# A two-layer attention, state-space and gated linear attention trunk: the first output projection in split fp32r products, its weights split in turns of the attention loop

## The reference, cut to what matters

```python
# layer 0
h = x @ w_in                                   # cq, ckv, k_rope, g_mla, u, g_s5
o_mla = mla_attention(...) * silu(g_mla)       # 8 heads, 512 channels, causal softmax
y = gelu(s5(u))
o_s5 = y * sigmoid(y @ w_glu + b_glu) * silu(g_s5)          # 256 channels
z = concatenate([o_mla, o_s5]) @ w_out         # 768 x 1024: the first output projection
x = layer_norm(ALPHA * x + z)
# layer 1
h = x @ w_in                                   # q, k, v, gk_low (16 columns), g
log_a = log_sigmoid(gk_low @ w_gk2 + b_gk) / 16             # the gate products, 16 x 512
o = rms_norm(chunked gated linear attention(q, k, v, log_a)) * silu(g)
x = layer_norm(ALPHA * x + o @ w_out)
```

## Time and profile before

| | us |
|---|---|
| median of 3 runs | 928.06 (923.01 to 928.16) |
| profiled execution | 926.22 |
| its span | 924.5 |
| attention turns 4 to 63 | from about 202 to 385 |
| first output projection | 385 to 475 |

### The profile page before, as it was taken

How to read it: one execution, slowest core, us unless ns; L and a number is a source line. 1 busy time by engine, 2 the same in 40 slices (tenths; PEclk the granted TensorE clock), 3 DMA queues, 4 the chain that set the end, 5 groups by cost and what they waited for, 6 DMA issues and landing times. The chain is left out here.

```text
span 924.5 us, 11820 instructions
## 1 busy us (share of the span) xinstructions
PE 892.7 (97%) x4384; PEld 691.5 (75%) x4384; DVE 448.1 (48%) x787; ACT 273.7 (30%) x536; POOL 222.0 (24%) x245
## 2 busy tenths in 40 slices
PE   7999999999999999999998999999999999999995
PEld 6888776766788777744455877888888888888884
DVE  5988689456666898344440433100000025554453
ACT  6152414553433344211113445002020326211120
POOL 2000002411110100544443230033413333142243
PEclk9999999999999999999999999999999999999998
DMA  9010255220000000522213110021001332021111
GB/s 338 11 28 23 72 84 121 85 76 2 1 1 1 1 1 13 170 77 83 91 57 103 46 46 1 11 86 52 23 23 50 98 114 92 23 81 57 46 48 67
DMA packets 34888, 55.61 MB, mean 60 GB/s; under 512 B 7664, under 2 KB 21232, under 8 KB 34816
## 3 DMA queue, kind: packets, MB, share of 16 engines
q1 hardware_dynamic: 34832, 54.87, 19.5%
HBM read 43.78 MB, written 9.44 MB: 58 GB/s over the span
## 5 line engine op out<-in xcount | busy, mean ns | idle before, releaser
L1521 DVE SCALAR_TENSOR_TENSOR w_out_lo<-w_out_raw,vecs,w_out_hi 128x1024 fp32r<-128x1024 f32 x8 | 10.5, 1314 | 161.8 <-ACT w_out_hi L1131 161.6
L1812 PEld LDWEIGHTS psum<-V,probT 128*128 128x128 f32 x576 | 69.3, 192 | 11.7 <-issue 8.1
L1812 PE MATMUL psum<-V,probT 128*128 128x64 f32 x576 | 74.4, 275 | 0.3 <-DVE rot L1468 0.3
L1675 PE MATMUL psum<-kT,qTt 96*128 96x512 f32 (+3 forms) x192 | 72.5, 487 | 1.2 <-DVE YT L612 1.2
L1063 ACT ACTIVATE prob<-psum,negmax 128x128 f32<-128x128 f32 (+7 forms) x64 | 47.4, 740 | 81.6 <-DVE negmax L1423 71.0
L1423 DVE TENSOR_REDUCE negmax<-psum 128x1 f32<-128x128 f32 (+7 forms) x64 | 48.5, 758 | 29.8 <-PE psum L1679 28.4
L1588 PE MATMUL psum<-w_out,OT 128*128 128x512 f32 x128 | 57.6, 593 | 0.0
L1588 PE MATMUL psum<-x1T_hi,wqk_hi 128*128 128x512 f32 x128 | 51.2, 400 | 0.0
L1588 PE MATMUL psum<-x1T_lo,wqk_hi 128*128 128x512 f32 x128 | 50.8, 397 | 0.0
L1588 PE MATMUL psum<-x1T_hi,wqk_lo 128*128 128x512 f32 x128 | 50.6, 395 | 0.0
L1588 PE MATMUL psum<-w_out_hi,Y1T_hi 128*128 128x512 f32 x128 | 50.6, 395 | 0.0
(11 more groups left out here) (349 smaller groups left out, 1923.7 us busy)
## 6 DMA issues: line engine op xcount, KB each, us to landing
wqk_raw<-odd_w_in_dram SPq DMA_DIRECT2D x8, 512.0 KB, 5.3
x_res<-x_dram SPq DMA_DIRECT2D x8, 512.0 KB, 3.4
x_scratch<-zn SPq DMA_DIRECT2D x8, 512.0 KB, 2.6
wv_raw<-odd_w_in_dram SPq DMA_DIRECT2D x16, 256.0 KB, 2.7
wg_raw<-odd_w_in_dram SPq DMA_DIRECT2D x16, 256.0 KB, 2.7
w_out_raw<-odd_w_out_dram SPq DMA_DIRECT2D x4, 1024.0 KB, 5.0
V<-x_scratch SPq DMA_DIRECT2D x8, 512.0 KB, 4.2
out_dram<-SG SPq DMA_DIRECT2D x8, 512.0 KB, 2.9
```

The costliest lines, as they stand in the source:

```text
L1521: step(vec.scalar_tensor_tensor(w_out1[2][:, k, :], w_out1[0][:, k, :], gla_c[:, 4 + k % 2:5 + k % 2], w_out1[1][:, k, :].bitcast(F32), AL ...
L1675: mm = pe.matmul(psum[:, slot + part, 0:c1 - c0], qTt[:, i % 2, h, :], kT[:, h, c0:c1], start=True, stop=not diag, skip_group_check=diag)
L1812: mm = pe.matmul(bank("o", i)[:, h * VD:(h + 1) * VD], lhsT, rhs, start=(k == 0), stop=(k == len(pairs) - 1))
```

## The change

The first output projection is made of three fp32r products for each f32 one. Its weights come in six loads of 128 rows; ScalarE copies each to hi and VectorE makes the low part, in turns 20, 24, 28, 32, 36 and 57. The operands, OT and the state-space output, are split tile by tile (`mix_hi_tile` on ScalarE, `mix_lo_tile` on VectorE). The sigmoid gates move from turns 44 to 59 to turns 4 to 19. The low-rank product has hi and lo of its weights side by side (32 columns), so two products instead of three; the gate product has its parts stacked on 96 rows, so one fp32r product instead of an f32 one. SyncE's loads of query and key weights and GpSimd's splits of them are in another order.

```diff
@@ sp
-            sp.dma_start(w_out0[:, :, :], even_w_out[0].rearrange("(k p) n -> p k n", p=P)).then_inc(w_out0_loaded, 16)
+            for k in range(1, 4):
+                w_out0_load(k, 0)
...
             sp.wait_ge(s5_states_set, 4)
+            sp.wait_ge(s5_out_set, 16)
+            for k in range(4, 6):
+                w_out0_load(k, 1)
             plan.filled(sp, ("q", NT - 1, 1))
-            sp.wait_ge(s5_out_set, 16)
+            sp.wait_ge(q_turned, NT)
+            w_out0_load(0, 2)
             wqk_load(0)
-            wqk_load(1)
...
             plan.filled(sp, ("z0", NT - 1, 1))
+            wqk_load(1)
+            plan.drained(sp, ("z0", NT - 1, 1))
@@ pool
-            for h in range(2):
-                wqk_split_head(h)
+            wqk_split_head(0)
...
+                if i == 1:
+                    pool.wait_ge(small_loaded, 16 * 3)
+                    step(pool.tensor_copy(gk2_parts[:, :], gk2[:, :]))
+                    step(pool.tensor_tensor(gk2_parts[4 * GR:6 * GR, :], gk2[4 * GR:6 * GR, :],
+                                            gk2_parts[4 * GR:6 * GR, :].bitcast(F32), ALU.subtract), gk2_split)
+            wqk_split_head(1)
@@ all
+        w_out0_turns = {20: (1, 0, 48), 24: (2, 0, 48), 28: (3, 0, 48), 32: (4, 1, 32), 36: (5, 1, 32), 57: (0, 2, 16)}
@@ scalar
+            def mix_hi_tile(i):
+                cols = slice(i * P, (i + 1) * P)
+                plan.drained(act, ("OT", i))
+                if i == 0:
+                    act.wait_ge(s5_out_set, 16)
+                if i >= 2:
+                    plan.filled(act, ("z0", i - 2, 1))
+                step(act.activation(mix_hi[i % 2][:, 0:4, :], OT[:, :, cols], ACT.Copy))
+                step(act.activation(mix_hi[i % 2][:, 4:6, :], gs5[:, :, cols], ACT.Copy), mix_hi_set)
...
+                    if n in w_out0_turns:
+                        k, batch, landed = w_out0_turns[n]
+                        act.wait_ge(w_out0_loaded[batch], landed)
+                        step(act.activation(w_out0_hi[:, k, :], w_out0_raw[k][:, :], ACT.Copy), w_out0_hi_set)
+            def low_hi(n):
+                s = slice(n * 512, (n + 1) * 512)
+                plan.filled(act, ("gk", n))
+                step(act.activation(low_parts[0:2 * GR, s], bank("gk", n)[0:2 * GR, :], ACT.Copy))
+                step(act.activation(low_parts[4 * GR:6 * GR, s], bank("gk", n)[0:2 * GR, :], ACT.Copy), low_hi_set)
@@ vector
+            def mix_lo_tile(i):
+                cols = slice(i * P, (i + 1) * P)
+                vec.wait_ge(mix_hi_set, i + 1)
+                step(vec.tensor_tensor(OT_lo[:, :, cols], OT[:, :, cols], mix_hi[i % 2][:, 0:4, :].bitcast(F32),
+                                       ALU.subtract))
+                step(vec.tensor_tensor(gs5_lo[:, :, cols], gs5[:, :, cols], mix_hi[i % 2][:, 4:6, :].bitcast(F32),
+                                       ALU.subtract), mix_split)
...
-                    if 44 <= n < 60:
-                        sigmoid_gate(n - 44)
+                    if 4 <= n < 20:
+                        sigmoid_gate(n - 4)
+                    if n in w_out0_turns:
+                        k = w_out0_turns[n][0]
+                        vec.wait_ge(w_out0_hi_set, sorted(w_out0_turns).index(n) + 1)
+                        step(vec.tensor_tensor(w_out0_lo[k][:, :], w_out0_raw[k][:, :], w_out0_hi[:, k, :].bitcast(F32),
+                                               ALU.subtract), w_out0_split)
...
+                elif what == "z0":
+                    mix_lo_tile(0)
...
+            mix_lo_tile(1)
             for i in range(NT + 1):
...
                     layer_norm(zn[:, i % 2, :], x_res[:, i % 2, :], "z0", i, i)
+                if i + 2 < NT:
+                    mix_lo_tile(i + 2)
@@ tensor
-                    pe.wait_ge(w_out0_loaded, 16)
-                    pe.wait_ge(s5_out_set, 16)
-                plan.drained(pe, ("OT", i))
+                    pe.wait_ge(w_out0_split, MIX // P)
+                pe.wait_ge(mix_split, i + 1)
...
-                          [(OT[:, k, ts] if k < 4 else gs5[:, k - 4, ts], w_out0[:, k, cs]) for k in range(6)])
+                          split_pairs([((mix_hi[i % 2][:, k, :], OT_lo[:, k, ts] if k < 4 else gs5_lo[:, k - 4, ts]),
+                                        (w_out0_hi[:, k, cs], w_out0_lo[k][:, cs])) for k in range(6)]))
...
-                group(("gate", m), bank("gate", m), [(gk2[:, h * P:(h + 1) * P], gkT[:, n * 512:(n + 1) * 512])])
+                group(("gate", m), bank("gate", m), [(gk2_parts[:, h * P:(h + 1) * P], low_parts[:, n * 512:(n + 1) * 512])])
```

More of the change, by code:

```diff
@@ L175, in hybrid_trunk @@
         gk2_at = cursor[0]
-        gk2 = own("gk2", [GR, GKW])
+        gk2 = own("gk2", [6 * GR, GKW])
         o = cursor[0]
@@ L265, in hybrid_trunk @@
         OT = at("OT", RB + 7424, [P, H * VD // P, S])
-        w_out0 = at("w_out0", RB, [P, MIX // P, D])
+        OT_lo = at("OT_lo", RB + 7424, [P, H * VD // P, S], F32R)
+        gs5_lo = at("gs5_lo", D6, [P, 2, S], F32R)
+        mix_hi = [at(f"mix_hi{s}", (RD + 8192, D5)[s], [P, MIX // P, P], F32R) for s in range(2)]
+        w_out0_hi = at("w_out0_hi", RB, [P, MIX // P, D], F32R)
+        w_out0_at = (RB + 6144, RT, RT + 1024, D1 + 2048, D7, D7 + 1024)
+        w_out0_raw = [at(f"w_out0_raw{k}", o, [P, D]) for k, o in enumerate(w_out0_at)]
+        w_out0_lo = [at(f"w_out0_lo{k}", o, [P, D], F32R) for k, o in enumerate(w_out0_at)]
         SGL = at("SGL", D7, [P, 4, 512])
@@ L340, in hybrid_trunk @@
         q_turned = sem("q_turned")
-        max_set, prob_set = sem("max_set"), sem("prob_set")
+        max_set = sem("max_set")
         gated = sem("gated")
-        w_out0_loaded, ln0_loaded = sem("w_out0_loaded"), sem("ln0_loaded")
+        w_out0_loaded, ln0_loaded = [sem(f"w_out0_loaded{s}") for s in range(3)], sem("ln0_loaded")
+        w_out0_split, mix_hi_set, mix_split = sem("w_out0_split"), sem("mix_hi_set"), sem("mix_split")
+        w_out0_hi_set = sem("w_out0_hi_set")
+        gk2_split, low_hi_set = sem("gk2_split"), sem("low_hi_set")
         xres_loaded = [sem(f"xres_loaded{s}") for s in range(2)]
@@ L870, in _, with split @@
                          s5_states_set if table is tabB else None)
+            def split(raw, hi, lo, signal):
+                step(pool.tensor_copy(hi, raw))
+                step(pool.tensor_tensor(lo, raw, hi.bitcast(F32), ALU.subtract), signal)
             pool.wait_ge(s5_n2_set, 4)
@@ L897, in _ @@
             pool.wait_ge(wgk_loaded, 16)
-            split(*(t[:, :, :] for t in w_gk), wgk_split)
-            for h in range(2):
-                wqk_split_head(h)
+            split(w_gk_raw[:, :, :], w_gk[:, :, 0:GR], w_gk[:, :, GR:2 * GR], wgk_split)
+            wqk_split_head(0)
             pool.wait_ge(ln0_loaded, 32)
@@ L1087, in _ @@
                     step(act.activation(stat[:, 20:21], stat[:, 1:2], ACT.Sqrt, bias=eps[:, 0:1]), root_set)
+                if i + 2 < NT:
+                    mix_hi_tile(i + 2)
                 if i == NT:
-                    plan.filled(act, ("gk", 0))
-                    step.frees(act.activation(gkT[:, 0:512], bank("gk", 0)[0:GR, :], ACT.Copy), ("gk", 0))
+                    low_hi(0)
                 if i:
@@ L1096, in _ @@
                              x1_hi_set)
-            plan.filled(act, ("gk", 1))
-            step.frees(act.activation(gkT[:, 512:1024], bank("gk", 1)[0:GR, :], ACT.Copy), ("gk", 1))
+            low_hi(1)
             for h in range(GH + 1):
@@ L1827, in low_rank @@
                 plan.claim(pe, ("gk", n))
-                group(("gk", n), bank("gk", n)[0:GR, :],
-                      split_pairs([([w[:, k, :] for w in w_gk[1:]], [x_[:, k, n * 512:(n + 1) * 512] for x_ in x1T])
-                                   for k in range(KD)]))
+                group(("gk", n), bank("gk", n)[0:2 * GR, :],
+                      [(w_gk[:, k, :], x_[:, k, n * 512:(n + 1) * 512]) for k in range(KD) for x_ in x1T])
             def gate_z(m):
@@ L1956 @@
     }
-    for name in ("mla_w_uq", "mla_w_ukv", "s5_w_glu", "even_w_out", "odd_w_in", "gla_w_gk2", "odd_w_out"):
+    laid_out["gla_w_gk2"] = np.tile(given["gla_w_gk2"][0], (6, 1))
+    for name in ("mla_w_uq", "mla_w_ukv", "s5_w_glu", "even_w_out", "odd_w_in", "odd_w_out"):
         laid_out[name] = given[name]
```

45 lines of the change are left out of this document (27 added, 18 removed).

## The result

The changed kernel takes 938.89 us (median of 4 runs, 934.09 to 940.72) beside 927.27 us of the kernel before (4 runs): 1.0126 times, 95% interval 1.0076 to 1.0177. Run again beside the experiments it gave 938.28 us and 1.0133 (1.0113 to 1.0153). So it is slower by 1.3%. The forecast was 930, the range 917 to 941; what came is the forecast's mechanism with the second rival, TensorE's clock, on top of it. The time is that rival's 938, and lies outside the 924 to 936 of the forecast as such. The profiled execution took 937.81 us, its span is 936.1.

A forecast was written before the change was run, and what follows sets the result against it. TensorE was taken to bound the kernel (busy 892.7 of 924.5 us), VectorE turns 4 to 19 after the change. On 926.2 us, terms 18.0 + 2.3 - 8.7 - 3.7 - 1.4 - 2.5 = +4.0 gave 930; range 917 to 941.

The forecast's parts named there:

- the forecast's mechanism: Turns 4 to 19: VectorE, filled by the moved gates, makes TensorE's V products wait; turn 19's 14.7 us later.
- the second rival: Turns 4 to 19: TensorE's clock falls to 1.2 GHz, +7 us at least, 938 us; chance 0.22.
- the forecast as such: Whole kernel: the expected outcome, 924 to 936 us; chance 0.60.
- What bounds, and where the gates cost: TensorE bounds the kernel; gates cost 0 in turns 44 to 59, but make VectorE the bound in turns 4 to 19.
- the attention, +18.0: Attention loop: early gates +16.4 us, weight splits of turn 24 +1.3 and turn 32 +0.3.
- VectorE, 16.4: Turns 4 to 21: gates in VectorE's queue delay turn 19's V product 14.7 us, turn 21's 16.4 in all.
- The weights, 1.6: Weight splits in the attention: turn 24 costs 1.3 us, turn 32 0.3 (between 0 and 1.3), turns 28, 36, 57 nothing.
- The projection's start, +2.3: Output projection, tiles 0 and 1: low parts in VectorE's queue delay the first layer norm, tile 2 starts 2.3 us later.
- Tiles 2 to 7, -8.7: Output projection, tiles 2 to 7: pitch 9.87 us set by VectorE instead of 11.17, 57.5 us against 66.2.
- The third rival: Output projection: GpSimd's layer norm holds VectorE twice per tile, pitch 12.2, 12 us more, 942 us; chance 0.08.
- Low-rank and gate products, -7.6: Behind the projection: low-rank products -3.7 us, stretch between second and query and key products -1.4, other four gate products -2.5.
- Early gates absorbed (0.10): Turns 4 to 19: the lead of four turns absorbs the gates, attention costs 4 instead of 18 us, 916; chance 0.10.

The follow-up runs named there:

- the last experiment: Kernel before, only its sixteen sigmoid gates moved from turns 44 to 59 to turns 36 to 39, 42 to 47 and 50 to 55: 926.52 us, 1.0008.
- the first: Kernel before, only its sixteen sigmoid gates moved from turns 44 to 59 to turns 4 to 19: 948.06 us, 1.0249.
- the kernel with late gates: Changed kernel with its sigmoid gates in turns 40 to 55, weight rows 4 and 5 loaded and split behind them: 918.91 us, 0.9924.
- The experiment with early tiles: Changed kernel with both halves of mixed-row tiles 0 and 1 made in turns 59 and 61: 934.73 us, 1.0088.
- the best version: Changed kernel, gates in turns 36-39, 42-47, 50-55, other weight-split turns, mixed-row tiles 0 and 1 before the loop's end, VectorE a turn after ScalarE: 908.93 us, 0.9808.

## Why the prediction was right, and where its sizes were wrong

**What bounds, and where the gates cost.** Right. That sixteen gates cost nothing in late turns of the kernel before is shown by the last experiment, that they cost more than 18 us in early ones by the first. That the time came out just at the second rival's 938 is luck: the clock cost less in these turns than the 7 us or more that the rival gave it, and the weights and the projection's start made up for it. VectorE's chain was sized well: turn 19's copy of probabilities was to end at 247.8 from a start at 201.99; with the clock kept whole it ends at 249.1 from 202.62, 0.7 us off.

**The step that was mis-sized: the attention, +18.0 against +25.4.** Three parts.
- *The clock, 0 against 4.6* (4.2 to 6.0 by the four traces that have these instructions). The second rival had its place and mechanism right, and its price (+7 at least) too high: it set slow work against the whole stretch of 45 us, but much of the slow time passes while TensorE waits for VectorE anyway. In the nine windows from 205 to 250 the clock withheld adds up to 13.6 us (5 us times 1 less the clock, each), and a third of it reached the end. I gave the rival 0.22, since the rows of before showed fuller stretches only, and made it hang on the busy share of a window. That does not decide: in the kernel with late gates the clock fell behind a window of 3.61 of 5 us, and in the kernel before it stayed at 1.00 behind the same window with the same rows. What the Trainium skill describes, "TensorE: Matmul & The Clock Gate" (the section "HAM oscillation — how this bites in real kernels"), a kernel that falls back to the slow clock by its waits between bursts, made this case the likelier one, and the changed kernel's trace agrees with it.
- *VectorE, 16.4 against some 17.4* (25.4 less the clock and the weights). The prediction let turn 19's V product follow its copy by 0.1 us. In the run it starts 3.1 us after that copy's end (249.1, 252.25): the last product that VectorE holds is turn 17's, and turns 18 and 19 follow at TensorE's own pace, 3.0 and 1.9 apart, as before. The sum counted two more turns of VectorE instead, which nearly makes up for it. That the binding wait is for qTt was not seen: I followed the copies of probabilities alone.
- *The weights, 1.6 against 3.4.* Turns 24 and 25 cost 1.3, as forecast. Turns 32 and 33 cost 2.1, taken at 0.3 with 1.3 as the bound. The row below has what was left out: VectorE waits for ScalarE's copy of the same turn, 1.28 us, before its own 1.23, and qTt is behind both.

```profile
286.65 1.23 DVE L1525 TENSOR_TENSOR w_out_lo<-w_out_raw,w_out_hi 128x1024 fp32r<-128x1024 f32 x1 [1.28 <-ACT w_out_hi L1122]
...
288.74 0.61 PE L1671 MATMUL psum<-ident,qt 128*96 128x128 f32 x4 [1.03 <-DVE qTt L1464]
```

**The projection's start, +2.3 against +4.5.** The chain was right: tile 0's low part, then tile 1's, then the first layer norm. It was costed at full clock, and from the start of the last V product to that of tile 0's first product it grew by 3.3 us (3.51 to 6.85), as forecast; but after the first two of its waits the clock fell (from 413.6 to 416.9 and from 427.4 to 430.8), and the products come 0.43 apart there instead of 0.23. The experiment with early tiles takes the first two of these waits away and 3.2 us net with them. The rows, against the earlier trace rows:

```profile
413.59 0.52 PE L1662 MATMUL psum<-w_out_hi,mix_hi 128*128 128x512 f32 x1 [3.17 <-issue]
...
414.34 0.63 PE L1662 MATMUL psum<-w_out_hi,OT_lo 128*128 128x512 f32 x1
414.77 0.63 PE L1662 MATMUL psum<-w_out_hi,mix_hi 128*128 128x512 f32 x1
...
426.12 0.50 PE L1662 MATMUL psum<-w_out_hi,mix_hi 128*128 128x512 f32 x1 [2.03 <-DVE gs_lo L1503]
...
437.91 1.09 PE L1671 MATMUL psum<-ident,zn 128*128 128x128 f32 x8 [1.72 <-POOL zn L926]
```

**Tiles 2 to 7, -8.7 against -9.9.** The chain bound where it was said to: in the middle tiles the pitch is 9.72 us against 9.87 (11.17 in the earlier trace rows), VectorE's queue sets it, and the new subtractions take 0.69 and 2.50 against 0.7 and 2.8. The terms listed for 9.87 add up to 10.0; to 9.9 without the 0.14, that is, if GpSimd's product starts when VectorE's first subtraction has ended. In the run it starts 0.11 us behind that subtraction's start and takes 0.4 us longer instead. The rest of the difference is at the ends: VectorE starts with slack, and the first and the last pitch are 9.13 and 9.24. Each of the two engines waited for the other where the other had begun (0.11 us were enough), VectorE for 2.1 us and GpSimd for 0.4; the rule of the Trainium skill, "SBUF — State Buffer" (the section "SBUF: two separate sides"), that the one of the two which starts first has the shared port for its whole instruction, says so, and the trace agrees in both directions. TensorE's own wait is only 0.3 to 0.5 us and for GpSimd, so that the wait of VectorE behind it is easily missed. The third rival, two holds of VectorE per tile and a pitch of 12.2, did not come.

**Low-rank and gate products, -7.6 against -8.1.** Right within 0.5, with the clock low after the gate products as before. That it might not fall there (2.5 us less) was among the outcomes of the forecast; most of the experiments show that, with 2.7 us.

**Early gates absorbed (0.10).** It fell twice: neither sixteen nor eight were.

## What to carry to other kernels

Slack of an engine that is read as a share of a stretch is not slack at a place: work put into an in-order queue costs what stands behind it and is waited for, here the copy of the next tile's queries, and by turn 19 half the work had cost half the time. Where one engine finishes what another has begun, look at what stands behind the second half: a wait of 1.3 to 1.7 us there cost TensorE two to four in two places and nothing in two others. A turn of delay between the halves is in the best version, which has no such wait, but was not tried by itself. And when a change makes TensorE wait, price the clock with it: not all slow time counts, but here it added a quarter to a third to what the waits themselves cost. Last, follow a small wait to its end before naming what binds: TensorE waited 0.4 us for GpSimd, GpSimd for VectorE, and VectorE for nobody but in the one operation that GpSimd blocked. And compare traces stage by stage before crediting an edit with a few microseconds, since a stage that it does not touch can change by as much.

## What the runs showed of the hardware

- More work made a stretch faster: 306 idle products in TensorE's waits kept the granted clock at 1.00 from 200 to 255 us and brought turn 19's V product 3.1 and 3.5 us nearer to turn 0's than in the changed kernel's two traces. The median fell by 3.9 us, of which not all need be the filler's, as said above.
- The same waits do not always bring the clock down. The rows of 210 to 215 us above are one case (0.66 with late gates, 1.00 before, the same work and wait ahead). Another: after the first gate products the changed kernel and the best version run the same instructions with nearly the same waits (1.90 and 0.50 us against 1.90 and 0.69); one falls to 0.50, the other stays at 1.00, and from the first gate product to the first V1 product it is 81.25 against 83.94 us. The windows, of the changed kernel and of the best version:

```profile
520.00:525.00 5.00, 4.50 (x11) 3.03 (x11) 0.26 (x2) 4.63 (x6) 4.71 (x5) 0.50 0.00 0
```

```profile
495.00:500.00 5.00, 4.30 (x20) 3.43 (x19) 0.17 (x2) 4.87 (x6) 4.71 (x5) 1.00 0.00 0
```

  So some 2.7 us of the best version's gain on the changed kernel came by how its waits happened to fall, and what decides that these runs do not tell. In all five of its runs the mean clock was 0.991 or more, so it was not one execution's luck.
- An engine that comes 0.11 us too late waits in full: the order in which VectorE's and GpSimd's operations start decides who is held. Both holds (0.4 us of GpSimd, 2.1 us of VectorE) are in the chain that sets the pitch; with both gone the five pitches after the first fall from 9.59 to 9.27 us on average, and TensorE's own work, 9.13 where it does not wait, is what remains.
